# Second layer's normed rows turned tile by tile while the first layer's expert outputs are added, with modulation columns by transposes, chunk squares summed by VectorE, and the slot list loaded and shifted at other places

## What is computed

```
for i in range(2):
    mod = silu(c) @ w_mod[i] + b_mod[i]          # and the same from c_ctx
    sh1, sc1, gt1, sh2, sc2, gt2 = split(mod, 6)
    h = rmsnorm(x, g_mix[i]) * (1 + sc1) + sh1
    cq, ckv = first columns of h @ w_in[i]       # 384 and 256 wide
    q  = rmsnorm(cq, g_q) @ w_uq;  kv = rmsnorm(ckv, g_kv) @ w_ukv
    ...                                          # three mixers, gates, w_out
    x = x + gt1 * y
    f = rmsnorm(x, g_ffn[i]) * (1 + sc2) + sh2
    x = x + gt2 * moe(f)                         # 64 experts, 8 chosen per token, + shared expert
```

## Time and profile before

| | us |
|---|---|
| median of 3 runs | 3370.18 |
| lowest and highest | 3364.9, 3371.2 |
| the profiled execution, its own time | 3383.25 |
| its span, first to last instruction | 3381.4 |
| PE busy | 3181.1 (94%) |
| DVE, ACT, POOL busy | 1745.9, 1336.9, 594.1 |

### The profile page before, as it was taken

One profiled execution on the slowest core, in us unless ns is written; L12 is line 12 of the kernel. 1 busy time (PEld: TensorE's weight loads), 2 busy tenths in 40 slices (PEclk: granted clock), 3 DMA queues, 4 the chain that ended last, 5 costly groups with the idle time before them and its releaser, 6 DMA issues.

```text
span 3381.4 us, 47597 instructions
## 1 busy us (share of the span) xinstructions
PE 3181.1 (94%) x14840; PEld 2225.7 (66%) x14840; DVE 1745.9 (52%) x2409; ACT 1336.9 (40%) x1883; POOL 594.1 (18%) x751
## 2 busy tenths in 40 slices
PE   6999999999998999999999699999998899999996
PEld 3457967899654766667676346876764576666662
DVE  1344252133265766676675525342425677676665
ACT  2244152212123555555554225342212455555551
POOL 0000310000043222222232000020004222233220
PEclk9989999999999999999999899999999999999999
DMA  6410212333515999999997910102240999999986
GB/s 220 126 63 7 78 32 76 131 131 131 202 40 203 370 377 362 361 372 385 377 376 265 373 52 1 54 20 89 88 151 29 344 374 356 351 365 358 345 318 250
DMA packets 224802, 727.19 MB, mean 215 GB/s; under 512 B 55890, under 2 KB 104660, under 8 KB 165396
## 3 DMA queue, kind: packets, MB, share of 16 engines
q1 hardware_dynamic: 179508, 633.37, 51.2%
q0 software_dynamic: 45184, 92.28, 7.3%
HBM read 707.64 MB, written 84.24 MB: 234 GB/s over the span
## 4 chain that ended last, share of the span: by engine, by line
PE 66%; DMA 19%; DVE 5%; issue 4%; ACT 3%; SPq 1%; another core or an unknown queue 1%; DVEq 0%; POOLq 0%; POOL 0%; ACTq 0%
PE ps L835 11%; PE ps L837 10%; PE ps L836 10%; PE ps L828 7%; DMA region_v<-in_w_exp_up 7%; PE ps L916 6%; PE ps L857 5%; PE ps L1025 5%; DMA ring<-in_w_exp_up 4%; PE ps L1127 4%; DMA region_k<-in_w_exp_up 4%; PE ps L1048 3%; DMA ring<-y_rows 2%; PE ps L944 1%; ACT region_h_split L1205 1%
## 5 line engine op out<-in xcount | busy, mean ns | idle before, releaser
L857 PEld LDWEIGHTS ps<-con,region_c 128*128 128x128 f32 x1878 | 249.1, 169 | 129.3 <-issue 96.5
L857 PE MATMUL ps<-con,region_c 128*128 128x128 f32 x1878 | 279.1, 278 | 23.2 <-DVE region_c L1818 10.5
L1983 POOL DMA_INDIRECT y_rows<-region_q,idx_out x141 | 142.4, 1010 | 896.0 <-DVE region_q L1587 805.1
L837 PE MATMUL ps<-region_x_split,ring_split 128*128 128x384 f32 (+2 forms) x800 | 282.8, 354 | 0.0
L835 PE MATMUL ps<-ring_split,region_q_split 128*128 128x512 f32 x568 | 227.8, 401 | 13.2 <-DVE ring_split L1554 12.9
L835 PE MATMUL ps<-region_h_split,region_q_split 128*128 128x512 f32 x560 | 224.4, 401 | 12.1 <-DVE ring_split L1554 11.3
L1205 ACT ACTIVATE region_q<-ps 128x512 f32<-128x512 f32 (+1 forms) x145 | 87.6, 604 | 359.8 <-PE ps L916 313.5
L837 PE MATMUL ps<-ring_split 128*128 128x512 f32 x568 | 222.5, 392 | 0.0
L837 PE MATMUL ps<-region_h_split,ring_split 128*128 128x512 f32 x560 | 219.4, 392 | 0.0
L1382 ACT ACTIVATE region_c<-ps 128x768 f32<-128x768 f32 (+1 forms) x48 | 33.8, 705 | 412.2 <-PE ps L837 412.2
L1205 ACT ACTIVATE region_c<-ps 128x512 f32<-128x512 f32 (+3 forms) x129 | 84.8, 657 | 225.6 <-PE ps L857 125.2
(11 more groups left out here) (312 smaller groups left out, 6915.6 us busy)
## 6 DMA issues: line engine op xcount, KB each, us to landing
ring<-in_w_mod SPq DMA_DIRECT2D x24, 2048.0 KB, 8.1
region_k<-in_w_exp_gate SPq DMA_DIRECT2D x48, 1024.0 KB
region_k<-in_w_exp_up SPq DMA_DIRECT2D x48, 1024.0 KB
region_k<-in_w_exp_down SPq DMA_DIRECT2D x48, 1024.0 KB
ring<-in_w_exp_gate SPq DMA_DIRECT2D x47, 1024.0 KB
ring<-in_w_exp_up SPq DMA_DIRECT2D x47, 1024.0 KB
ring<-in_w_exp_down SPq DMA_DIRECT2D x47, 1024.0 KB
region_v<-in_w_exp_gate SPq DMA_DIRECT2D x46, 1024.0 KB
```

The lines of the kernel that those rows point to most:

```text
L837: last = mm(o, wl, xh, start=False, stop=k == len(stationary) - 1)
L857: last = nc.tensor.transpose(ps[0:t.shape[1], at:at + t.shape[0]], t, ident[0:t.shape[0], 0:t.shape[0]])
L1983: pool.indirect_dma_start(Y8, bass.IndirectOffsetOnAxis(ap=idx_out[:, s:s + 1], axis=0), yb[:, s, :], None, bounds_check=TOK * TOPK - 1, o ...
```

## The change

What it does:

1. **mod**: the `sel2` matmuls give way to four transposes of the same 128x128 pieces; DVE adds the four groups (a reduce of 4x2x4 values per partition), waits for itself, and adds the bias.
2. **Squares**: DVE adds the chunk squares (two adds for `cq`, one for `ckv`), and `rq` and `rk` have one matmul per half in place of three and two.
3. **Layer 1's `h` jobs are gone.** In layer 0's `combine`, PE turns tile i-1 (8 transposes into `slot[2]`) right behind its sum for tile i, ACT evicts tile t-1 with scale and shift (8 activations of 128x128) ahead of its square of tile t; of the last tile, ACT evicts four chunks and DVE four. `XN_next` holds two tiles in `Q`, and the third buffer of `half_b` moves from `HT` to pieces of `Q` and `C`.
4. **Slot list**: in both layers SP issues the list's load behind expert 0's three weight loads, not ahead of them. In layer 1 DVE shifts the list ahead of `first`.
5. Some semaphores are merged; `sg` now waits for all three shared-expert loads, which were issued by 904 us, 72 us ahead of the first `sg`.

```
-        for k in range(DK):
+        for k in range(DK if l == 0 else 0):
             add("h", l, k, drain=alt[k % 2])
...
+        if ahead:
+            add("shift", l)
         add("first", l)
         shared(("sg", -1))
-        if ahead:
-            add("shift", l)
-        else:
+        if not ahead:
...
-                sp.wait_ge(sl["listed"], 16 * TOPK * len(A))
-                sp.dma_start(slots, LISTS[l].rearrange("(p n) a -> p (n a)", p=P)).then_inc(sl["list_in"], 16)
                 sp.wait_ge(tab_ready, l + 1)
...
                 load_gate_up(expert(0), 0)
                 load_down(expert(0), 0)
+                sp.wait_ge(sl["listed"], 16 * TOPK * len(A))
+                sp.dma_start(slots, LISTS[l].rearrange("(p n) a -> p (n a)", p=P)).then_inc(sl["list_in"], 16)
...
+            def turn_next(l, t):
+
+                pe.wait_ge(xn_ready, NT * (l + 1) + t + 1)
+                if t:
+                    pe.wait_ge(h_evicted, t)
+                turn(slot[2], [(k * P, XN_next[:, t % 2, k * P:k * P + P]) for k in range(DK)]).then_inc(h_turned, 1)
...
-                    for j in range(4):
-                        last = mm(ps[:, 2 * j:2 * j + 2], modrow(*a)[:, j * P:j * P + P], cst("sel2"), start=True, stop=True)
+                    last = turn(ps, [(j * P, modrow(*a)[:, j * P:j * P + P]) for j in range(4)])
...
-                    cs = (0, 1, 2) if kind == "rq" else (3, 4)
-                    after(pe, *(("cq", l, 2) if kind == "rq" else ("ckv", l, 1)))
-                    last = project(ps, [cst("ones") for _ in cs], [sq[:, i, :] for i in cs], full(l, kind) or kind == "rk")
+                    i = 0 if kind == "rq" else 3
+                    pe.wait_ge(squares_added, 2 * l + (2 if kind == "rq" else 1))
+                    last = project(ps, [cst("ones")], [sq[:, i, :]], full(l, kind) or kind == "rk")
...
                         last.then_inc(b_summed, 1)
+                        if l < DEPTH - 1 and i:
+                            turn_next(l, i - 1)
+                    if l < DEPTH - 1:
+                        turn_next(l, NT - 1)
...
+                        def evict(t, ks):
+                            act.wait_ge(h_turned, t + 1)
+                            s = 0 if t >= CT else 1
+                            for k in ks:
+                                ins = A_(hT[:, k, t * P:t * P + P], slot[2][:, k * P:k * P + P], ACT.Identity,
+                                         scale=column(l + 1, "A1", s, k), bias=column(l + 1, "sh1", s, k))
+                            ins.then_inc(h_evicted, 1)
+
+                        act.wait_ge(setup_dve, 2 * l + 3)
                         for t in range(NT):
+                            if t:
+                                evict(t - 1, range(DK))
                             act.wait_ge(combined, t + 1)
                             A_(junk, XT[:, t, :], ACT.Square, accum_out=ssq[:, t:t + 1]).then_inc(pre_ssq, 1)
                             act.wait_ge(pre_var, NT * l + t + 1)
                             A_(rstd[:, t:t + 1], ssq[:, t:t + 1], ACT.Sqrt).then_inc(pre_rstd, 1)
-                            if t < 4:
-                                normed(t)
-                        act.wait_ge(combined, NT)
-                        for t in range(4, NT):
                             normed(t)
+                        evict(NT - 1, range(DK // 2))
...
+                if l < DEPTH - 1:
+                    dve.wait_ge(h_turned, NT)
+                    for k in range(DK // 2, DK):
+                        ins = ts(hT[:, k, TOK - P:TOK], slot[2][:, k * P:k * P + P], column(l + 1, "A1", 0, k),
+                                 column(l + 1, "sh1", 0, k), ALU.mult, ALU.add)
+                    ins.then_inc(h_evicted, 1)
```

More of the change, by code:

```diff
@@ L429, in build @@
         half_a = [ring[:, 4096 * i:4096 * i + 4096] for i in range(3)]
-        half_b = [w[:, 0:4096] for w in (K, VY, HT)]
+        half_b = [[K[:, 0:2048], K[:, 2048:4096]], [VY[:, 0:2048], VY[:, 2048:4096]], [Q[:, 2048:4096], C[:, 0:2048]]]
+        XN_next = Q[:, 0:2048].rearrange("p (a d) -> p a d", a=2)
         PS = stack.enter_context(nc.psum_tensor("ps", [P, 4096], F32))
@@ L454, in build @@
         max_ready, exp_ready, o_full, o_drained = sem("max_ready"), sem("exp_ready"), sem("o_full"), sem("o_drained")
-        rd_ready = sem("rd_ready")
+        h_turned, h_evicted = sem("h_turned"), sem("h_evicted")
+        rd_ready, squares_added = sem("rd_ready"), sem("squares_added")
         sink_sum, sink_exp = sem("sink_sum"), sem("sink_exp")
@@ L966, in _ @@
                     rows = ROPE if kind == "kr" else P
-                    after(pe, "h", l, DK - 2)
-                    after(pe, "h", l, DK - 1)
+                    if l == 0:
+                        after(pe, "h", l, DK - 2)
+                        after(pe, "h", l, DK - 1)
+                    else:
+                        pe.wait_ge(h_evicted, NT + 1)
                     last = project(ps, [w[:, k, col:col + rows] for k in range(DK)], [hT[:, k, :] for k in range(DK)],
@@ L1015, in _ @@
                             pe.wait_ge(kk_ready, l + 1)
-                            pe.wait_ge(kk_zero, l + 1)
+                            pe.wait_ge(zeroed, 2 * l + 2)
                             after(pe, "vs", l)
@@ L1141, in _ @@
                     l, t = a
-                    pe.wait_ge(s_sgu, 32 * (l + 1))
+                    pe.wait_ge(s_shared, 48 * (l + 1))
                     w = w_sgu.rearrange("p (g k n) -> p g k n", g=2, k=DK)
@@ L1153, in _ @@
                     l, t = a
-                    pe.wait_ge(s_sd, 16 * (l + 1))
+                    pe.wait_ge(s_shared, 48 * (l + 1))
                     w = chunks(w_sd, 2, D)
@@ L1191, in _ @@
                             for half in range(2):
-                                at = D * j + 512 * half
-                                last = mm(slot[i % 2][:, 512 * half:512 * half + 512], ident, half_b[i % 3][:, at:at + 512],
+                                at = D * (j % 2) + 512 * half
+                                last = mm(slot[i % 2][:, 512 * half:512 * half + 512], ident, half_b[i % 3][j // 2][:, at:at + 512],
                                           start=j == 0, stop=j == TOPK // 2 - 1)
                         last.then_inc(b_summed, 1)
+                        if l < DEPTH - 1 and i:
+                            turn_next(l, i - 1)
+                    if l < DEPTH - 1:
+                        turn_next(l, NT - 1)
                 if job.drain:
@@ L1364, in _ @@
                     act.wait_ge(roped, roped_no(l, "s"))
-                    act.wait_ge(u_zero, l + 1)
+                    act.wait_ge(zeroed, 2 * l + 1)
                     copy(KK[0][0][0:64, :], KS[0:64, :])
@@ L1661, in _ @@
                     b4 = vecT[:, l * NVEC + V_B + 4 * a[1]:l * NVEC + V_B + 4 * a[1] + 4]
-                    last = tt(modT[:, at:at + 8].rearrange("p (j s) -> p j s", s=2),
-                              ps[:, 0:8].rearrange("p (j s) -> p j s", s=2), b4.unsqueeze(2).broadcast_to([P, 4, 2]), ALU.add)
+                    parts = ps[:, 0:512].rearrange("p (j g r) -> p j r g", j=4, g=4)[:, :, 0:2, :]
+                    now = modT[:, at:at + 8].rearrange("p (j s) -> p j s", s=2)
+                    link(vec.tensor_reduce(now, parts, AX.X, ALU.add))
+                    last = tt(now, now, b4.unsqueeze(2).broadcast_to([P, 4, 2]), ALU.add)
                     if a[1] in (3, 11):
@@ L1681, in _ @@
                                   ALU.mult, ALU.add)
+                elif kind in ("cq", "ckv") and a[1]:
+                    after(dve, *((kind,) + a))
+                    first, ev = 3 if kind == "ckv" else 0, full(l, kind)
+                    total = sview(sq[:, first, :], ev)
+                    ins = tt(total, total, sview(sq[:, first + a[1], :], ev), ALU.add)
+                    if a[1] == (1 if kind == "ckv" else 2):
+                        ins.then_inc(squares_added, 1)
+                    else:
+                        link(ins)
                 elif kind in ("rq", "rk"):
@@ L1900, in _ @@
                 gp.memset(KK[0][1], 0.0)
-                gp.memset(K[:, 0:4 * UW], 0.0).then_inc(u_zero, 1)
-                pool.wait_ge(u_zero, l + 1)
+                gp.memset(K[:, 0:4 * UW], 0.0).then_inc(zeroed, 1)
+                pool.wait_ge(zeroed, 2 * l + 1)
                 pool.wait_ge(kk_ready, l + 1)
-                gp.memset(KK[1][1][0:64, :], 0.0).then_inc(kk_zero, 1)
-                pool.wait_ge(kk_zero, l + 1)
+                gp.memset(KK[1][1][0:64, :], 0.0).then_inc(zeroed, 1)
+                pool.wait_ge(zeroed, 2 * l + 2)
                 lo, hi = (0, UW) if l < DEPTH - 1 else (UL - 8, UW)
```

12 lines of the change are left out of this document (6 added, 6 removed).

## The result

| | before | after |
|---|---|---|
| median of 6 runs, us | 3369.95 | 3382.21 |
| lowest and highest | 3364.9, 3371.9 | 3378.5, 3388.7 |
| the profiled execution: own time, span | 3383.25, 3381.4 | 3378.58, 3376.8 |

The ratio is 1.0042, with a 95% interval from 1.0031 to 1.0053: the changed kernel is slower by some 14 us. The two profiled executions don't show that. The one of before lay above all six of its runs, the one of after was the fastest but one. So the spans are not compared here, only stretches, and where it matters the same stretch in several kernels.

The account below looks back on a forecast made before the run. PE, busy for 94% of the span, was taken as the bound. Modulation -8.8, squares -5.5, tail +27.2 and list +2.0 made +14.9 us, carried over to 3370.18 as 3385; 8 in 10 range 3370 to 3395.

Parts of the forecast that it names:

- the likeliest case: Whole kernel: tail later with a low clock, gains as summed; 3377 to 3392 us, chance 0.70.
- The ring: Layer 0's tail: turn, mean, add and sum wait in a circle; period 13.6 against 9.94 us, 14.6 us later.
- The clock in the ring: Layer 0's tail: PE's pauses lower its clock, lengthening four sums with their turns by 2.4 each, 9.6 us.
- the granted clock would be near 0.5 at each turn: Layer 0's tail: a sign expected in the new trace, granted clock near 0.5 at each turn.
- The tail's end: Layer 0, last add to first projection: 13.6 us against 13.1 before, 0.5 us later.
- First matmuls at a low clock: First projection after layer 0's tail: it comes after a pause, so low clock costs 2.5 us.
- The list: Layer 1's routing: slot list behind expert 0's loads delays the split; expert 0's first product comes 2.0 us later.
- Squares: `rq` and `rk` in both layers: fewer matmuls, gain 5.5 us, bounds 4 and 7.
- Modulation: The 24 `mod` jobs: shorter by transposes, gain 9.0 - 0.2 us, bounds 5 and 12.
- a merge stretch shorter by 4 us: Merge stretch (530 to 880 us): the forecast would be wrong if it isn't shorter by 4 us.
- the "faster" rival: Layer 0's tail: turning hides, no sum waits, 9.94 us a tile kept; -9.3 us, 3361; chance 0.06.
- The gather of layer 0: Layer 0's routing: rival that the gather is late among the weights, 5 us, 3390; chance 0.05.

Follow-up runs that it names:

- run 5: The changed kernel with 6 matmuls of 512 columns, result unread, ahead of each of the six turns in layer 0's tail; ratio to before 0.9999.
- run 1: The changed kernel with the mean of tile i-1 moved on VectorE ahead of its wait for TensorE's sum i; ratio to before 0.9960.
- run 4: The changed kernel with 12 matmuls of 512 columns, result unread, ahead of each of the six turns in layer 0's tail; ratio to before 1.0079.
- run 2: The changed kernel with before's tail (eight `h` jobs, `XN` and `half_b`) put back; ratio to before 0.9975.
- run 6: The kernel before with only the modulation columns done by transposes; ratio to before 0.9987.
- run 7: The kernel before with only the sums of squares added by VectorE; ratio to before 0.9987.
- run 3: The kernel before with only the tail's part of the change; ratio to before 1.0065.
- run 8: The changed kernel with the mean moved ahead of VectorE's wait and the slot list loaded ahead of expert 0's weights; ratio to before 0.9938.
- run 9: The kernel of run 8 with four matmuls of 512 columns, result unread, ahead of the last turn alone; ratio to before 0.9959.
- run 10: The kernel of run 8 with each of the merge's modulation turns issued three times; ratio to before 0.9972.

## Why the prediction was right

Forecast 3385, measured 3382.21, slower, within the likeliest case. The mechanism in the tail and at the list was right. The sum had luck too: falls of the clock outside the tail, which no term held, moved single stretches by 1.7 to 5.1 us and nearly cancelled. Its terms one by one, the measured ones from the stretches:

**The ring.** Forecast: period 13.6, 14.6 us in all. Shown by run 5 at 13.54 against 9.94: 4 x 3.60 = 14.4. Run 1 opens it and the delay is gone.

**The clock in the ring.** Forecast 9.6, four times 2.4. The four periods of after are 15.58, 16.31, 15.00 and 16.02, together 62.9, less 4 x 13.54: 8.7. Against the rule of the Trainium skill weighed there ("TensorE: Matmul & The Clock Gate", Part 4: PE-mode transpose) the trace speaks once more. By it each sum would begin with the whole rise still ahead and cost 3.2; the one behind the turn of 1900.53 took 7.65, only 0.6 over the 7.03 of the full clock. The mean of 2.2 alone wouldn't decide, since the pause was shorter than the 9.6 us that the 3.2 were read behind. I had said that the granted clock would be near 0.5 at each turn, and it is 0.50 in all six; the turns' 1.97 us, double the 1.04 and 1.09 of runs 4 and 5, says the same.

**The tail's end.** Forecast 0.5 more than the 13.1 of before. From the end of the last add, 1928.59 + 1.23, to 1942.99 it is 13.2: 0.1. C in all is 99.7 and 99.3 against 76.5 to 78.0 (mean 77.3 of before and runs 2, 6, 7): 22.2, where ring, clock and end made 24.7.

**First matmuls at a low clock.** Forecast 2.5. Among the nine kernels with squares by VectorE D differs by up to 5.8 us, and that is the clock. Busy time of D in after and in run 7 (PE, granted clock, DMA share, GB/s):

```profile
1943.00:2050.00 107.00, 99.77 (x249) 0.95 0.19 47
```

```profile
1945.80:2047.00 101.20, 93.94 (x249) 1.00 0.20 50
```

PE is busy for most of D, so its length times its mean granted clock, an estimate from the clock's record in each trace, tells what it would take at the full clock. That is 101.1 to 101.2 in all nine kernels with squares by VectorE, and 103.2 to 103.4 in the three without. In after the clock stays at 0.50 until 4.9 us after the first projection starts, which costs half of that, 2.4: as forecast. Runs 1 and 3 have 4.8 and 3.7 us of it, runs 5, 8, 9 and 10 some 3, and before and runs 2, 4, 6 and 7, with the 48 transposes or a full fill ahead, none. Behind later waits of D the clock falls twice in after and once in before; that one more costs 1.7, and nobody forecast it.

**The list.** Forecast 2.0. The split starts 10.6 to 10.8 us after the gate load in the five kernels with the late list and 8.4 to 8.7 in the seven with it early: 2.2. E is 26.7 in the mean of the five, 24.0 in the mean of the seven: 2.7, of which the rest, 0.5, lies behind the split's start. Mechanism as told, size somewhat low.

**Squares.** Forecast 5.5: `rk` 1.35 twice, `rq` 1.8 and 1.05. A falls by 3.0 in run 7 (1.35 + 1.8 = 3.15 was meant), or by 2.8 as length times clock. D, taken the same way, falls by 2.1 against 2.4. About 5.

**Modulation.** Forecast 8.8. What a job saves was set low: 0.33, where it is 0.46 in most places. But "these jobs stand among PE's own work (12 in the merge, which PE fills)" left two things out. Some of the eleven end in a wait that takes the saving up, and the clock fell where it hadn't fallen before. So the merge gave 0.4 in place of 3.6, and my own sign for this, a merge stretch shorter by 4 us, failed at once. Row L835 behind L1662 in the waits of before, 0.5 twice, was the trace of the waits, and I hadn't looked at what a shorter job would run into. By length times clock B is 322.8 in the mean of the eight and 326.0 in the mean of the three, 3.2 less: the work was saved, and the clock took most of it back. Ahead of the merge it went the other way. There eight jobs of 0.46 make 3.7, A is 3.8 shorter in run 6 by length times clock, and 5.6 as read. From the eighth to the tenth row job, before and run 6:

```profile
202.50:252.80 50.30, 48.02 (x373) 0.93 0.20 64
```

```profile
198.40:244.70 46.30, 43.78 (x363) 1.00 0.21 69
```

The clock falls twice there in before and in run 7 and once in run 3, and in none of the nine kernels with transposes; PE's waits there are the same to 0.3 us. Again no run shows why. The 2.4 at the start isn't settled: the first projection begins at 48.1 to 51.5 in nine kernels with transposes and at 48.8, 52.8 and 53.8 in three without.

**The sum.** The tail, less 1 by which C was shorter in fact, is 14.4 + 8.7 + 0.1 - 1 = 22.2. First matmuls 2.4 and the list 2.7 come on top. Squares and modulation together take 5.8 in A (the two alone took 2.8 and 3.8), 3.2 in B and 2.1 in D, by length times clock: 11.1. That makes 16.2, or 14.1 with the 2.1 by which the start's means differ. The clock's other falls, in the traces of before and after, make -5.1 in A, +1.7 in B and +1.7 in D, together -1.7. The ratio says 14 (10 to 18), and the 12.3 us between the medians is within that. The forecast's 14.9 holds a tail that is 2.5 too dear and gains that are about 1 too large: with the list's 0.7 these errors nearly made up for each other.

**The rivals.** The turning could not hide as the order was, but it can: run 1 is the "faster" rival made true, with the point from which it decides (the wait of turn i-1 ends before sum i does) nearly met. The gather of layer 0 was not late: in the first 60 us from the first expert product on PE waits 1.8 and 0.3 us in before and the same in after.

## What to carry to other kernels

When work is spread into a loop that overlaps, follow one item round through every engine's program order: a one-line helper left behind the wrong wait (here the mean behind the next tile's add) closed a ring that cost 23 us, and moving it made the same change 13 us faster than before in place of 14 slower. Before a saving on the busiest engine is counted, look at what its next instruction waits for, and at the granted clock of the same stretch in several traces: here 4.8 us of saved work showed as 0.4, with 1.8 gone to waits and 2.7 to the clock. Where PE is busy nearly throughout, a stretch's length times its mean granted clock takes the clock out of the comparison. And an engine that pauses for 5 us pays again behind the pause (2.2 us for a turn and a sum here), so a ring is dearer than its length.

## What of the hardware was not expected

Single executions of the same code differ in one stretch by nearly as much as the change is worth. From the first output product of layer 0 to the first expert product it took 182.1 us in after and 194.5 in run 1, with the same program there. Busy time of that stretch, after and run 1 (PE, PEld, DVE, ACT, POOL, granted clock, DMA share, GB/s):

```profile
865.90:1048.00 182.10, 172.69 (x539) 85.91 (x540) 95.04 (x282) 38.78 (x58) 58.21 (x66) 0.97 0.35 128
```

```profile
870.30:1064.80 194.50, 175.31 (x540) 87.08 (x540) 95.20 (x282) 38.82 (x58) 57.79 (x66) 0.94 0.33 120
```

The granted clock differs, 0.97 against 0.94, but PE was busy only 2.6 us longer. The rest of the 12.4 us is waiting, and two waits in run 1's timeline of PE make up most of it:

```profile
1007.38 0.48 PE L1182 MATMUL ps<-onesb,Mb 128*64 128x1 bf16 x6 [3.77 <-DVE region_c L1860]
1014.45 0.69 PE L859 MATMUL ps<-con,region_c 128*128 128x128 f32 x2 [6.59 <-DVE region_c L1860]
```

In after, the same two rows wait for nothing and for 0.54 us. VectorE waits there for ACT's part of two `sg` jobs (L1424). In run 1 these start 17.0 and 24.0 us after the first of their rows on PE (989.46), in after 7.2 and 14.0 us (985.07). The stretch is 182 to 186 us in seven of the twelve traces and 193 to 195 in five (runs 1, 3, 7, 8 and 10). What makes the difference stays open.

The profiled span of after came out 4.6 us below that of before although the kernel is 14 us slower. The largest part of that is one stretch in which PE's program is the same, from layer 1's first scores to expert 0's gate load: 574.9 us in before, 564.0 in after, 569.0 to 575.1 in the others. PE's 2946 rows there take 551.75 us in before, at a mean granted clock of 0.98, and 544.69 in after, at 1.00. A single profile can't show a change of this size in its span.
